# Order of the projection's tiles and the decay rows of the state-space scan in one step of a hybrid decoder layer

## The reference, cut to what matters

```python
cum = jnp.cumsum(dt * a, axis=2)                     # within chunks of 128 positions
seg = cum_t[..., :, None] - cum_t[..., None, :]
decay = jnp.exp(jnp.where(causal, seg, -jnp.inf))
cb = jnp.einsum('bcign,bcjgn->bcgij', cm, bm)
y_diag = jnp.einsum('bcgeij,bcjgep->bcigep', cb[:, :, :, None] * decay, xdt)
states = jnp.einsum('bcjgn,bcjgep->bcgepn', bm, xdt * decay_end[..., None])
h = exp(cum_last) * h + states                       # chunk after chunk
y_off = jnp.einsum('bcign,bcgepn->bcigep', cm, h_prev) * jnp.exp(cum)[..., None]
y = y_diag + y_off                                   # plus D * x, times SiLU(z)
```

## Time and profile before

| what | value |
|---|---|
| median of the runs | 1980.32 us |
| the profiled execution: its own time | 1976.95 us |
| its span, first to last instruction | 1974.8 us |
| PE busy (matmuls) | 1764.8 us, 89% |
| DVE, ACT, POOL busy | 960.3, 674.7, 651.4 us |
| mean granted clock of PE | 0.933 of full speed |
| projection stage (0 to 304 us), scan stage (304 to 498 us) | 304, 194 us |

### The profile page before, as it was taken

One profiled execution on the slowest core, in us unless ns is written; L12 is line 12 of the kernel. 1 busy time (PEld: TensorE's weight loads), 2 busy tenths in 40 slices (PEclk: granted clock), 3 DMA queues, 4 the chain that ended last, 5 costly groups with the idle time before them and its releaser, 6 DMA issues. The chain is left out here.

```text
span 1974.8 us, 35021 instructions
## 1 busy us (share of the span) xinstructions
PE 1764.8 (89%) x13258; PEld 1590.1 (81%) x13258; DVE 960.3 (49%) x1605; ACT 674.7 (34%) x1336; POOL 651.4 (33%) x382
## 2 busy tenths in 40 slices
PE   6999986888799799879997796897998799999999
PEld 6999984555799799646665695896888799999999
DVE  4307886889521254237773212533223468788400
ACT  4443333333431242135551222315332333333221
POOL 2344432443334233114441242001223333434343
PEclk9999996788899899879998898998999999999999
DMA  4222212221322333212003221451533222222233
GB/s 134 75 88 92 75 53 100 94 93 65 112 80 85 130 96 123 89 39 91 1 0 100 85 93 64 151 190 61 229 127 117 97 65 95 85 96 85 80 94 117
DMA packets 58067, 185.03 MB, mean 94 GB/s; under 512 B 6694, under 2 KB 19366, under 8 KB 54566
## 3 DMA queue, kind: packets, MB, share of 16 engines
q1 hardware_dynamic: 56822, 181.91, 27.8%
q10 hardware_dynamic: 1168, 2.08, 0.3%
HBM read 166.08 MB, written 22.07 MB: 95 GB/s over the span
## 5 line engine op out<-in xcount | busy, mean ns | idle before, releaser
L254 POOL TENSOR_TENSOR mm_ring<-mm_raw,mm_ring 128x1024 fp32r<-128x1024 f32 x94 | 230.0, 2449 | 530.9 <-ACT mm_ring L231 361.5
L264 PE MATMUL up_pp<-h,mm_ring 128*128 128x260 f32 x2016 | 243.9, 284 | 3.0 <-POOL mm_ring L254 3.0
L264 PEld LDWEIGHTS up_pp<-h,mm_ring 128*128 128x128 f32 x2016 | 243.8, 189 | 3.2 <-ACT up_conv_s L2782 3.2
L264 PE MATMUL ssd_pp<-h,ssd_ring 128*128 128x260 f32 x1920 | 237.3, 285 | 9.2 <-POOL ssd_ring L254 9.2
L264 PEld LDWEIGHTS ssd_pp<-h,ssd_ring 128*128 128x128 f32 x1920 | 234.0, 190 | 12.1 <-issue 8.9
L231 ACT CAST mm_ring<-mm_raw 128x1024 fp32r<-128x1024 f32 x106 | 111.1, 1050 | 339.3 <-PE up_pp L264 228.8
L264 PE MATMUL up_pp<-act_t,mm_ring 128*128 128x260 f32 x1344 | 163.5, 284 | 6.8 <-POOL mm_ring L254 6.8
L264 PEld LDWEIGHTS up_pp<-act_t,mm_ring 128*128 128x128 f32 x1344 | 163.1, 190 | 7.1 <-issue 7.1
L254 POOL TENSOR_TENSOR ssd_ring<-mixed,ssd_ring 128x1024 fp32r<-128x1024 f32 x42 | 104.5, 2491 | 179.6 <-ACT ssd_ring L231 162.9
L264 PE MATMUL nq_pp<-h,nq_ring 128*128 128x260 f32 x960 | 122.2, 288 | 10.4 <-POOL nq_ring L254 10.4
L264 PEld LDWEIGHTS nq_pp<-h,nq_ring 128*128 128x128 f32 x960 | 119.2, 192 | 11.3 <-issue 10.6
(11 more groups left out here) (433 smaller groups left out, 3098.9 us busy)
## 6 DMA issues: line engine op xcount, KB each, us to landing
mm_raw<-in_w_up SPq DMA_DIRECT2D x44, 512.0 KB, 3.6
mixed<-in_w_ssd SPq DMA_DIRECT2D x42, 512.0 KB, 3.6
mem_ring<-in_mem_kv SPq DMA_DIRECT2D x16, 1024.0 KB, 6.4
ms_raw<-in_w_ssd_merge SPq DMA_DIRECT2D x24, 512.0 KB, 3.6
mm_raw<-in_w_mkv_qm SPq DMA_DIRECT2D x24, 512.0 KB, 3.6
nq_raw<-in_w_qk SPq DMA_DIRECT2D x20, 512.0 KB, 3.7
mixed<-in_ssd_state SPq DMA_DIRECT2D x16, 512.0 KB, 3.6
out_s_ssd<-mixed SPq DMA_DIRECT2D x16, 512.0 KB, 2.6
```

Of the source, the lines that this page charges most:

```text
L254: pool.tensor_tensor(self.ring[:, u, 1], self.raw[:, u], self.ring[:, u, 0].bitcast(F32), ALU.subtract).then_inc(self.low, 1)
L264: last = pe.matmul(out(n), self.ring[:, b % 2, wn, k], x[:, xn, chunk + k, part], start=start and k == 0 and wn + xn == 0, stop=stop and k ...
```

## The change

**Tiles.** The order becomes: dt, gates, 6 z tiles, 4 x tiles, and then five times x, x, z, x, x, z. The weights are laid out in that order on the host (`tile_order`). ACT's program is written accordingly: `z_tile` and `x_tile` hold what a tile needed before, the lead is written out, the sixes are a loop. DVE convolves in the same order.

**Running sums.** They are kept in fp32 in one part, written to DRAM once (`cum_rows`, on ACT's queue), and for each step SP loads the 8 rows of 128 of its group and chunk, broadcast to all 128 partitions, into a ring `seg` of four (512 KB a step). POOL adds the mask there (`hide_future`) in place of the copies and selectors; PE's products with selectors and mask go, and it reads B, C and x from `xbct`. ACT exponentiates `seg` in place.

**Moved work in the scan.** ACT makes x times dt (`take_front`; line 971 on DVE before) and the product with D (`times_d`; part of line 1007 before); DVE adds the transposed y in one operation. The outer products `xb` lie in PSUM, two buffers of two, and `step` takes them pair by pair. PE waits for the product's own `ready` only after `front` and `turn_y`. All 16 steps are written out for every engine. The diff, cut:

```diff
+            for n in range(Z_FIRST):
+                z_tile(1 + n // 2, n % 2, n)
+                if n == 3:
+                    steps.act_c(act)
             steps.act_d(act)
-            some_z(5, first_x)
+            for t in range(X_FIRST):
+                x_tile((2 + Z_FIRST + t) // 2, t % 2, t, t % 2)
+                if t:
+                    silu(t - 1, (t - 1) % 2)
+            silu(X_FIRST - 1, 1)
+            def six(g, last):
+                i, t, n = g * 3 + lead // 2, g * 4 + X_FIRST, g * 2 + Z_FIRST
+                x_tile(i, 0, t, 0)
+                x_tile(i, 1, t + 1, 1)
+                silu(t, 0)
+                z_tile(i + 1, 0, n)
+                silu(t + 1, 1)
+                x_tile(i + 1, 1, t + 2, 0)
+                x_tile(i + 2, 0, t + 3, 1, last)
+                silu(t + 2, 0)
+                z_tile(i + 2, 1, n + 1, last)
+                silu(t + 3, 1)
+            tile_loop(act, 0, rounds, six)
...
-        do(dve.tensor_copy(low_high[H:, :], pct[H:, :]))
-        dve.tensor_copy(cumt[0:H, :], pct[0:H, :])
-        dve.tensor_tensor(cumt[H:, :], pct[H:, :], low_high[H:, :].bitcast(F32), ALU.subtract).then_inc(ready, 1)
+        dve.tensor_copy(cumt[:], pct[0:H, :]).then_inc(ready, 1)
         dve.wait_ge(exped, 1)
+        act.dma_start(self.d["cum_rows"].rearrange("k (h i) -> h k i", h=SSD_HEADS),
+                      self.cumt[:].rearrange("h (k i) -> h k i", k=TT)).then_inc(self.rows_stored, 16)
...
-        seg = s.sb("sc_seg", [P, HPG, P])
+        seg = s.sb("sc_seg", [P, AHEAD, HPG, P])
+        xb = s.ps("sc_xb", [P, 2, 4, STATE])
...
+            def load_rows(v):
+                g, k, _ = where(v)
+                sp.dma_start(seg[:, v % AHEAD].rearrange("p a b -> p (a b)"),
+                             d["cum_rows"][k:k + 1, g * HPG * P:(g + 1) * HPG * P].broadcast_to([P, HPG * P])).then_inc(rows_landed[v % AHEAD], 16)
+            for v in range(TT):
+                load_rows(v)
+                sp.dma_start(ring[:, v], of_state("ssd_state", v)).then_inc(landed[v], 16)
+            for v in range(STEPS):
+                if v + AHEAD < STEPS:
+                    sp.wait_ge(ready, v + 1)
+                    load_rows(v + AHEAD)
+                sp.wait_ge(read_out, v + 1)
+                sp.dma_start(of_state("out_s_ssd", v), ring[:, v % TT]).then_inc(stored[v % TT], 16)
+                if v + TT < STEPS:
+                    sp.wait_ge(stored[v % TT], 16 * (v // TT + 1))
+                    sp.dma_start(ring[:, v % TT], of_state("ssd_state", v + TT)).then_inc(landed[v % TT], 16)
...
+            def hide_future(v):
+                pool.wait_ge(rows_landed[v % AHEAD], 16 * (v // AHEAD + 1))
+                pool.tensor_tensor(seg[:, v % AHEAD], seg[:, v % AHEAD],
+                                   c["ssd_mask"][:].unsqueeze(1).broadcast_to([P, HPG, P]), ALU.add).then_inc(masked, 1)
...
+            diagonals(0)
+            hide_future(0)
+            hide_future(1)
+            diagonals(1)
+            for v in range(STEPS):
+                if v:
+                    gate(v - 1)
+                scale(v)
+                if v + 2 < STEPS:
+                    hide_future(v + 2)
+                    pool.wait_ge(on_rows, v + 1)
+                    diagonals(v + 2)
+            gate(STEPS - 1)
...
+            def front(v):
+                g, k, pos = where(v)
+                b, cc = xbct[:, DI + g, pos], xbct[:, DI + GROUPS + g, pos]
+                if v:
+                    pe.wait_ge(ready, v)
+                pe.matmul(pcb[:, 0, :], b, cc, start=True, stop=True)
+                pe.transpose(pcb[:, 1, :], b, c["ident"][:])
...
+            def rows_of_sample(v):
+                pe.wait_ge(diag_ready, v + 1)
+                if v:
+                    pe.wait_ge(read_out, v)
...
+                if v + 1 < STEPS:
+                    front(v + 1)
+                if v:
+                    turn_y(v - 1)
+                    pe.wait_ge(state_done, v)
+                pe.wait_ge(ready, v + 1)
...
+            def times_d(v):
+                g, k, pos = where(v)
+                if v >= 2:
+                    act.wait_ge(gated, v - 1)
+                for j in range(XC):
+                    ins = act.activation(yx[:, v % 2, j, :], xbct[:, g * XC + j, pos], ACT.Copy,
+                                         scale=c["ssd_d"][:, g * XC + j:g * XC + j + 1])
+                ins.then_inc(weighed_d, 1)
+            def decays(v):
+                g, k, _ = where(v)
+                act.wait_ge(masked, v + 1)
+                for e in range(HPG):
+                    at_e = seg[:, v % AHEAD, e, :]
+                    ins = act.activation(at_e, at_e, ACT.Exp, bias=negcum[:, k, g * HPG + e:g * HPG + e + 1])
+                ins.then_inc(exped, 1)
+            def take_front(v):
+                g, k, _ = where(v)
                 act.wait_ge(fronted, v + 1)
-                act.copy(br[:, k % 2, :], pcb[:, 1, :])
+                if v >= 2:
+                    act.wait_ge(multiplied, v - 1)
+                act.copy(br[:, v % 2, :], pcb[:, 1, :])
                 for e in range(HPG):
-                    ins = act.activation(seg[:, e, :], pbc[:, e, :], ACT.Exp, bias=negcum[:, k, bass.ds(g * HPG + e, 1)])
-                ins.then_inc(exped, 1)
-            def outers(g, k, first=False):
-                v = g * TT + k
+                    ins = act.activation(xdt[:, v % 2, e, :], px[:, e, :], ACT.Copy,
+                                         scale=dtr[:, k, g * HPG + e:g * HPG + e + 1])
+                ins.then_inc(taken, 1)
...
+                    q = v * PAIRS + n // OUT
+                    if n % OUT == 0 and q >= 2:
+                        act.wait_ge(stepped, q - 1)
+                    ch = (k % 2) * HC + n
+                    ins = act.activation(xb[:, q % 2, n % OUT, :], pbs[:, 0, n // (HC // G2)], ACT.Copy,
+                                         scale=xdt_s[:, ch, g * 2 + k // 2:g * 2 + k // 2 + 1])
+                    if n % OUT == OUT - 1:
+                        ins.then_inc(outer, 1)
...
+            outers(0)
+            take_front(0)
+            decays(0)
+            for v in range(STEPS):
+                if v + 1 < STEPS:
+                    take_front(v + 1)
+                    decays(v + 1)
+                times_d(v)
+                if v + 1 < STEPS:
+                    outers(v + 1)
...
+            def weigh(v):
+                dve.wait_ge(taken, v + 1)
+                dve.tensor_tensor(xend[:, v % 2], px[:], of_heads(wend, v), ALU.mult)
                 dve.wait_ge(exped, v + 1)
-                dve.tensor_tensor(m[:, k % 2], seg[:], pcb[:, 0, :].unsqueeze(1).broadcast_to([P, HPG, P]),
...
+                    q = v * PAIRS + n // OUT
+                    if n % OUT == 0:
+                        dve.wait_ge(outer, q + 1)
+                    ch, col = (k % 2) * HC + n, g * 2 + k // 2
+                    ins = dve.scalar_tensor_tensor(out=ring[:, v % TT, n, :], in0=ring[:, v % TT, n, :],
+                                                   scalar=dxs[:, ch, 1, col:col + 1], in1=xb[:, q % 2, n % OUT, :],
+                                                   op0=ALU.mult, op1=ALU.add)
+                    if n % OUT == OUT - 1:
+                        ins.then_inc(stepped, 1)
...
+            def add_dx(v):
                 dve.wait_ge(turned, v + 1)
-                if late:
-                    dve.wait_ge(gated, v - 1)
-                for j in range(XC):
-                    ins = dve.scalar_tensor_tensor(out=yx[:, k % 2, j, :],
-                                                   in0=at(xbct, g * XC + j)[:, k * P:(k + 1) * P],
-                                                   scalar=at(c["ssd_d"], g * XC + j), in1=pt[:, j, :],
-                                                   op0=ALU.mult, op1=ALU.add)
-                ins.then_inc(gained, 1)
-            def take_in(g, k):
-                v = g * TT + k
+                dve.wait_ge(weighed_d, v + 1)
+                dve.tensor_tensor(yx[:, v % 2], yx[:, v % 2], pt, ALU.add).then_inc(gained, 1)
...
+            for v in range(STEPS):
+                if v == 0:
+                    step(0)
+                    read_state(0)
+                    weigh(0)
+                    weigh(1)
+                else:
+                    step(v)
+                    add_dx(v - 1)
+                    read_state(v)
+                    if v + 1 < STEPS:
+                        weigh(v + 1)
+                take_in(v)
+            add_dx(STEPS - 1)
...
+def tile_order():
+    z, x = [2 + n for n in range(DI)], [2 + DI + n for n in range(XBC)]
+    order = [0, 1] + z[:6] + x[:4]
+    for g in range(5):
+        a, b = 4 + 4 * g, 6 + 2 * g
+        order += [x[a], x[a + 1], z[b], x[a + 2], x[a + 3], z[b + 1]]
+    return order
```

(77 more changed lines are left out.)

322 lines of the change are left out of this document (112 added, 210 removed).

## The result

The changed kernel takes **1923.88 us** (median of 4 runs, 1921.86 to 1925.50) against 1980.26 for the kernel before beside it: ratio 0.9715, 95% interval 0.9698 to 0.9732. I had forecast 1935.0 and a range of 1924 to 1955: the direction is right, the gain is 11 too small, and the time lies 0.1 under the low end of the range. The profiled execution took 1924.66 (span 1922.8, against 1974.8).

A forecast was written before the change was run, and what follows sets the result against it. PE bounds the z tiles, DVE the convolved tiles and the scan. Gains of 13.0 (projection), 30.3 (scan steps) and 2.0 (head) sum to 45.3: 1976.95 becomes 1931.65, plus 3.4 to the median, forecast 1935.0, range 1924 to 1955.

The forecast's parts named there:

- Projection, 13.0 forecast: Projection stage: the new tile order gains 7.2 at PE's last tile and 5.8 in the tail, 13.0 us.
- The 2.5 "lost, once" in the lead: Projection lead: PE waits once for a cast behind the fourth convolved tile's SiLU, 2.5 us lost, bounds 0 and 5.8.
- The tail: Projection end: last SiLU comes 3.9 after PE's last tile instead of 9.7, since that tile is z; 5.8 us gained.
- DVE paces this part: Projection, tiles with a convolution: PE waits through POOL and ACT for DVE's convolution, so tiles take 6.48 each.
- My rule for collisions: DVE and POOL exclude each other when DVE reads two SBUF operands, and do not when one comes from PSUM.
- DVE's step, 30.3 forecast: Scan: 14 steps take 128.5 (11 of 9.31, three of 8.7) against 158.85, a gain of 30.3 us.
- the wait for pairs, +0.4: Scan step: DVE's update pairs three and four wait for ACT to fill buffers, +0.4 estimated, bounds 0 and 1.1.
- Head of the scan, 2.0: Scan start until the second step: about 22 instead of 24.2, 2.0 us gained, bounds +3 and -4.
- The low clock: Rival, scan: PE at 1.2 GHz becomes the bound, steps of 10.0, gain 24.5 instead of 30.3, 1941; chance 0.11.
- The convolution that keeps the pace: Rival, projection: ACT's order holds PE in every six, only the tail's 5.8 is won, 1942; chance 0.07.
- The collision: Rival, scan: updates still collide with POOL despite a PSUM operand, up to 2.39 in 14 steps, +33.5, 1968.5; chance 0.04.
- the 6.8 where they would have decided: Rival, scan: broadcast rows choke the DMA, deciding from a row load of 6.8 (13.0 a step); 1989, chance 0.05.

The follow-up runs named there:

- the control: The changed kernel itself, unedited, run again beside three edits of it, against the kernel before: 1923.87 us, ratio 0.9726 (0.9713 to 0.9739).

## Why the prediction was right, and where it was wrong

*Projection, 13.0 forecast, 19.5 in the trace.* This is the step that failed, with two terms of its sum. The 2.5 "lost, once" in the lead never came: I chained four convolutions at "the present 6.48" (my own times, 119.6 and 122.4, even give 2.8), and in the lead, written out, they follow PE's 5.77. The tail gave 8.55 (9.7 to 1.15) where I took 5.8: I left the last convolution late by several us, and it was in time. It took 4.0 (275.82 to 279.83), for POOL's last subtraction was over at 271.9. PE's last tile ends 10.95 earlier (290.75 and 279.8) where I had 7.2; besides the 2.5, 1.2 of that lies ahead of the cast at 106.88 (108.07 before) and is scatter, as the control's 108.37 shows. From that cast on the projection gives 18.3 in both traces of the changed kernel, 5.3 over the forecast.

Behind both terms stands one wrong price. That "DVE paces this part" held for the loop of before, where DVE waits for ACT only ahead of its first convolution (49.6 of 49.6). But 6.48 is the pace of that loop, and I carried it to convolutions outside it. It held 1.04 of idle time of the loop's own and 1.8 behind POOL (busy 5.36, where the same operations undisturbed add up to 3.56); written out the two are 0.18 and 1.5. In the sixes, which are a loop still, a convolution costs DVE 6.7 (busy 6.1, idle 0.64, over 20 of them), no less than before. There the forecast was right: four times 6.7 is 27, and PE's six tiles leave 34.6. So the order pays by the room that it gives a slow loop, 17.1 when it comes alone. Beside convolutions that are written out it is worth only its tail: in the old order the kernel is then 3.8 behind the control by medians, 4.0 by spans.

*My rule for collisions was too narrow.* I had DVE and POOL exclude each other only where DVE reads two operands in SBUF. In the kernel before, line 594, which reads one operand of 8 columns, stretches as well (timeline, DVE and POOL):

```profile
155.38 2.41 POOL L254 TENSOR_TENSOR ssd_ring<-mixed,ssd_ring 128x1024 fp32r<-128x1024 f32 x1 [3.36 <-ACT ssd_ring L231]
...
155.67 2.15 DVE L594 TENSOR_SCALAR ssd_acc<-ssd_acc,c_rest 128x8 f32<-128x8 f32 x1
```

Its median of 0.23 becomes 2.15, until POOL is done. In the sixes of the changed kernel that line takes 1.18 on average, and the copy of the tails (0.17 alone) 0.89. The Trainium skill ("SBUF — State Buffer", SBUF: two separate sides) gives the port pair to whichever begins first for a whole instruction, and names, beside operations with two SBUF inputs, those in a two-port mode. The trace agrees that a one-input operation can be held for POOL's whole instruction; which mode line 594 ran in, no run here shows.

*DVE's step, 30.3 forecast, 32.3 in the trace.* Right, with one term mis-sized: the regular step of 9.31 was 9.13, mainly since the wait for pairs, +0.4, was 0.15. The three steps that begin a group average 8.72 as forecast at 8.7, but one by one they are 8.41, 9.27 and 8.48, so that this average is in part luck. Putting the products with D back costs 0.43 a step, the very term of the sum. Of the 32.3, 19.6 are waits (158.85 less 14 times 9.95), for y above all, and they are gone; since front, selectors and the wait for `ready` were changed at once, which of these edits took them away was not tested.

*Head of the scan, 2.0.* The second step starts 22.1 after the first transfer (284.22), forecast 22. What I left out is the last step: 12.0 here (432.86 to the end) against 11.3 before, but 10.2 in the control. TensorE's clock makes that difference, as the rivals show.

*From the profiled execution to the median.* I added the 3.4 by which the median stood above it. Four sets of runs of the kernel before have medians from 1976.76 to 1980.26, and the control's profiled run equals its median: the offset was scatter, and cost 4 of the 11 missed. Without it the forecast would have been 1931.65, and the range would have begun near 1920.

*The rivals.* The low clock did not set the steps: the mean granted clock in the scan rose from 0.77 to 0.83 (from the second step on, from 0.80 to 0.86) though PE has less to do, and behind the head PE waits for DVE's product for 1.4 at most and for its y for up to 2.7. It did come in two places. Between the stages PE stands still for 5.7 (until 285.53) and in the head for 8.7 (until 297.79), and the granted clock is 0.50, the lower level, from 288 to 300. And in the last step of the changed kernel's first trace it is 0.50 from 437 to 445, where the control's trace has 1.00 until 439.7. PE's products within the chunk in that step, in the first trace and then in the control's:

```profile
435.91 3.68 PE L935 MATMUL sc_pyd<-sc_xdt,sc_m 128*128 128x64 f32 x16
```

```profile
437.83 2.00 PE L935 MATMUL sc_pyd<-sc_xdt,sc_m 128*128 128x64 f32 x16 [0.93 <-DVE sc_yx L1046]
```

DVE waits 1.39 for them in the first and not at all in the control. In both, PE had waited 2.71 for y just before (ahead of 432.40 and of 434.32); why the clock fell in one only stays open. The Trainium skill ("TensorE: Matmul & The Clock Gate", Why this matters for your kernels) warns of idle gaps between bursts of products. The trace agrees as to the head. I had used its rule for gaps of any length, which made 1941, and that is not borne out: 1923.88, and 0.86 over the steps. The convolution that keeps the pace fell with PE's gapless row. The collision does not come with the products in PSUM, and costs 3, not 33.5, with them in SBUF. The rows land in 4.9, well under the 6.8 where they would have decided, and doubling them changes nothing. The 23 us that I estimated from the Trainium skill ("SBUF — State Buffer", A bandwidth-pool intuition that's wrong), should all copies hang on one memory port, did not come: the same 4.9 excludes it.

## What to carry to other kernels

A pace read in a loop that is bound by an engine is not that engine's price: it holds the loop's own idle time and the collisions that this phase brings, so look at the idle time before each line first, and try the loop written out before reordering the work (here that alone gave 13.9, the order alone 17.1). Moving an operation off the bounding engine pays only as far as the next chain allows; find that chain's end (here ACT's decays, which came 0.56 late for DVE) and move it in the same edit. Size a change from the profiled execution and keep the distance to the median for the range, not for the forecast.

## What was not expected of the hardware

A DVE operation of 3 columns can cost nearly as much as POOL's whole instruction (2.4): in the run with the tiles alone the copy of the tails took 2.32 in place of 0.17 once in the lead, with the next convolution back in step, and 2.2 seven more times in the sixes. And a broadcast that reads one row of 4 KB 128 times lands 512 KB in 4.9, 0.8 over a state of that size (4.1), while the twelve extra ones took 5.7 and delayed no one.
